# First norm of a two-block transformer kernel: weight row read from PSUM, real products ahead of the turns, shared squares

## The chip, the cores and the metric

The kernel runs on one core of one Trainium2 chip. The metric is device time in microseconds, launch to end. The kernel before took 901.84 us (median of 3 runs, 901.46 to 902.21).

## The reference, cut to what matters

The whole program computes two stacked blocks on x of 512 tokens by 1024 channels, in float32. Only its first step bears on the change:

```
def rms_norm(x, gain, eps=1e-6):
    y = x * rsqrt(mean(x * x, axis=-1, keepdims=True) + eps)
    return y * gain

h = rms_norm(x, pre_norm_gain)       # 512 x 1024, gain: one row of 1024
proj = h @ w_in                      # 1024 x 4096, eight parts of 512 columns
q, k, v, z_a, b_gate, c_gate, u, z_c = split(proj, 8)
...                                  # differential attention, gated convolution,
                                     # output product, norms, a gate, then a second block
```

The part v is computed first, because it is wanted with tokens on the partitions.

## The kernel before, in words

**Numbers in two halves.** Every large product is made nearly exact with three products of rounded operands: each operand is split into a high half (fp32r) and a low half (the rest). The helper `exact` (L2033) issues high x high, high x low and low x high into one PSUM bank. A block of k tiles of 128 channels is therefore 3k matmuls of 128x128 by 128x512.

**Weights.** They come in units of 2048 columns per partition, each in two halves of 1024. SyncE loads the halves into `raw`; GpSimd (POOL) makes `whi` by a copy (L836) and `wlo` by a subtraction (L843), two instructions of 512 columns each for a half. For the very first half ScalarE makes `whi` instead (L964). `w_lo` counts halves whose low part is ready. There are two slots for split units, so POOL waits for TensorE to finish with unit n before it splits unit n+2.

**The first stage.** x is loaded in four tiles of 128 tokens (`x_load`, L690), in between the first weight halves: x0, w0, x1, x2, w1, x3, w2, w3. Per tile t:

- ScalarE squares both halves of 512 channels with a row sum (`square_x`, L956, instruction L942).
- POOL adds the two sums and raises to -1/2 (`root`, L781; L791 and L794), giving `rstd`.
- VectorE multiplies x by `rstd` and by the gain row in one instruction a half (`normed_x`, L1422; L1428) into `tok`, which holds two tiles in turn.
- TensorE turns `tok` with four transposes a half into a PSUM bank (`turn`, L2108; L2120), so that channels lie on the partitions.
- ScalarE copies the bank to `actA_hi` (`turned`, L945; L953), and VectorE writes the rest to `actA_lo` (`rest`, L1383; L1394). `lo["x"]` counts these.
- TensorE computes the block of v for the tile. It is cut in three: `("Th", "v", 0, 0, t)`, the first two channel tiles of weight unit 0, whose weights are split first; `("T", "v", 0, 0, t)`, the other two, which need the second half of the unit; and `("T", "v", 0, 1, t)`, four channel tiles of unit 1.

**The gain row.** ScalarE's first instruction loads the row of `pre_norm_gain` to one partition (L961). TensorE spreads it to 128 partitions by a product with a row of ones, one matmul with one row for each half (`gn`, L2209), and VectorE copies the two PSUM banks to `gain[:, 0]` (L1419). Only then does it norm. Between, TensorE does twelve transposes of the identity (`warm`, L2212), whose result is used by nothing.

**Order.** Each engine works in program order. TensorE's is the list of `tensor_order` (L188): blocks wait for what `ready` (L2123) names, and for the bank to be emptied (`bank_of`, L253, and `emptied`, L555). In the first stage it is: gn0, gn1, warm, and per tile the two turns, then from tile 2 on `T` of tile t-2, then `Th` of tile t; after that T of tiles 2 and 3, the four blocks of unit 1, and the blocks for q and k. POOL's order is: root 0; low part of half 0; root 1; high part of half 1; root 2; its low part; root 3; the halves of unit 1; and so on. VectorE's and ScalarE's orders are written out in the code below. A memset of two pad columns (L1409) raises `pads_made`, which ScalarE waits for when it copies the first convolution input.

## Time and profile before

| | |
|---|---|
| median of 3 runs | 901.84 us |
| profiled execution | 902.16 us |
| its span, first to last instruction | 900.4 us |
| mean granted TensorE clock | 0.993 |
| TensorE busy | 875.2 us, 97% |
| VectorE, ScalarE, GpSimd busy | 542.6, 356.4, 556.4 us |
| in the first 2 to 14 us: TensorE, VectorE busy | 10.99, 8.52 us |

The profile is one execution. Engines are PE (matmul), PEld (its weight load), DVE (VectorE), ACT (ScalarE), POOL (GpSimd) and SP (SyncE). A line as L843 is a line of the kernel; a helper's line stands for all its callers. "out<-in" names the tiles. In a timeline the bracket at the end says how long the engine was idle before the instruction and what released it. Matmuls overlap, so the distance between two starts, and not the duration, is what one costs.

### The profile page before, as it was taken

The page shows a single profiled execution, that of the slowest core. Times are in us where ns is not written, and L with a number is a line of the kernel's source. Part 1 is how long each engine was busy: PE and PEld are TensorE (multiplying, and loading weights), DVE is VectorE, ACT ScalarE, POOL GpSimd, SP SyncE. Part 2 cuts the span into 40 slices and gives each one's busy share as a digit, 9 for nine tenths or more (in the row PEclk, how much of TensorE's full clock was granted, in tenths as well). Part 3 has the DMA queues.
Part 4 walks back from the last instruction along what each step waited for, and adds up shares of the span by engine and source line. Part 5 has one row for each costly group of instructions (what it writes and reads, how often), then busy time and mean ns, then how long its engine had stood idle before and what let it go on. Part 6 is the DMA issues. An engine that isn't in the chain of part 4 may idle for free.

```text
span 900.4 us, 11943 instructions
## 1 busy us (share of the span) xinstructions
PE 875.2 (97%) x4224; PEld 727.0 (81%) x4224; DVE 542.6 (60%) x878; ACT 356.4 (40%) x792; POOL 556.4 (62%) x620
## 2 busy tenths in 40 slices
PE   8999999999999999999999999999977999999997
PEld 5888888888888777888888888888866988888886
DVE  6125647775035489676766625556975457878624
ACT  5124332431134367545112311123634436766622
POOL 7766556576789832318974058762397798556352
PEclk9999999999999999999999999999998999999999
DMA  7443231332422467895742254327932122211202
GB/s 198 140 129 103 71 91 50 94 140 89 133 83 94 142 129 164 212 219 167 175 126 90 75 165 122 111 94 178 223 115 69 47 95 71 71 48 62 80 1 94
DMA packets 81516, 102.65 MB, mean 114 GB/s; under 512 B 11825, under 2 KB 54321, under 8 KB 81458
## 3 DMA queue, kind: packets, MB, share of 16 engines
q1 hardware_dynamic: 72752, 85.12, 29.5%
q0 software_dynamic: 8704, 16.78, 11.0%
q8 instruction: 34, 0.56, 0.3%
q14 instruction: 24, 0.20, 0.1%
q10 hardware_dynamic: 2, 0.00, 0.0%
HBM read 99.79 MB, written 2.10 MB: 113 GB/s over the span
## 4 chain that ended last, share of the span: by engine, by line
PE 90%; POOL 5%; issue 2%; DVE 1%; ACT 1%; DMA 0%; POOLq 0%; DVEq 0%; ACTq 0%
PE bank L2036 27%; PE bank L2037 27%; PE bank L2038 27%; PE bank L2264 2%; PE bank L2292 1%; PE bank L2120 1%; POOL wlo L843 1%; PE bank L2237 1%; PE bank L2287 1%; PE bank L2286 1%; POOL tok L813 1%; POOL raw L813 1%; DVE tok L1428 1%; POOL v5lo L843 1%; ACT junk L942 1%
## 5 line engine op out<-in xcount | busy, mean ns | idle before, releaser
L843 POOL TENSOR_TENSOR wlo<-raw,whi 128x512 fp32r<-128x512 f32 x204 | 280.8, 1407 | 0.1
L836 POOL TENSOR_SCALAR whi<-raw 128x512 fp32r<-128x512 f32 x202 | 141.8, 738 | 185.4 <-PE bank L2038 176.4
L2036 PE MATMUL bank<-actB_hi,whi 128*128 128x512 f32 (+1 forms) x416 | 159.5, 383 | 2.3 <-POOL wlo L843 2.3
L2037 PE MATMUL bank<-actB_lo,whi 128*128 128x512 f32 (+1 forms) x416 | 158.6, 381 | 0.0
L2038 PE MATMUL bank<-actB_hi,wlo 128*128 128x512 f32 (+1 forms) x416 | 158.5, 381 | 0.0
L2036 PE MATMUL bank<-whi,actA_hi 128*128 128x512 f32 x320 | 128.5, 402 | 6.7 <-DVE wlo L1702 5.0
L2037 PE MATMUL bank<-wlo,actA_hi 128*128 128x512 f32 x320 | 126.2, 394 | 0.0
L2038 PE MATMUL bank<-whi,actA_lo 128*128 128x512 f32 x320 | 126.2, 394 | 0.0
L2036 PEld LDWEIGHTS bank<-actB_hi,whi 128*128 128x128 f32 x416 | 78.2, 188 | 17.5 <-issue 2.9
L2038 PEld LDWEIGHTS bank<-actB_hi,wlo 128*128 128x128 f32 x416 | 78.2, 188 | 15.1
L2037 PEld LDWEIGHTS bank<-actB_lo,whi 128*128 128x128 f32 x416 | 78.3, 188 | 14.1
L2036 PE MATMUL bank<-actA_hi,whi 128*128 128x512 f32 x224 | 87.9, 392 | 0.0
L2037 PE MATMUL bank<-actA_lo,whi 128*128 128x512 f32 x224 | 87.3, 390 | 0.0
L2038 PE MATMUL bank<-actA_hi,wlo 128*128 128x512 f32 x224 | 87.3, 390 | 0.0
L2036 PEld LDWEIGHTS bank<-whi,actA_hi 128*128 128x128 f32 x320 | 61.0, 191 | 21.5 <-DVE wlo L1702 5.2
L2038 PEld LDWEIGHTS bank<-whi,actA_lo 128*128 128x128 f32 x320 | 61.1, 191 | 13.1
L2037 PEld LDWEIGHTS bank<-wlo,actA_hi 128*128 128x128 f32 x320 | 61.1, 191 | 12.4 <-issue 0.2
L2036 PE MATMUL bank<-whi,actB_hi 128*128 128x512 f32 x144 | 56.4, 392 | 0.0
L2038 PE MATMUL bank<-whi,actB_lo 128*128 128x512 f32 x144 | 56.1, 390 | 0.0
L2037 PE MATMUL bank<-wlo,actB_hi 128*128 128x512 f32 x144 | 56.0, 389 | 0.0
L1735 DVE TENSOR_TENSOR acc<-acc,gcv 128x512 f32<-128x512 f32 x16 | 15.6, 972 | 58.4 <-ACT gcv L1213 58.4
L2038 PEld LDWEIGHTS bank<-actA_hi,wlo 128*128 128x128 f32 x224 | 42.0, 188 | 8.9
(262 smaller groups left out, 1593.7 us busy)
## 6 DMA issues: line engine op xcount, KB each, us to landing
raw<-in_a_w_in SPq DMA_DIRECT2D x44, 512.0 KB, 4.3
raw<-in_w_in SPq DMA_DIRECT2D x32, 512.0 KB, 3.8
raw<-in_b_w_in SPq DMA_DIRECT2D x16, 512.0 KB, 3.4
raw<-in_a_w_out SPq DMA_DIRECT2D x12, 512.0 KB, 3.4
gain<-in_a_w_out POOLq DMA_DIRECT2D x9, 512.0 KB, 8.6
raw<-in_w_out SPq DMA_DIRECT2D x8, 512.0 KB, 4.0
raw<-in_w_ple_gate SPq DMA_DIRECT2D x8, 512.0 KB, 3.3
gain<-in_a_w_in POOLq DMA_DIRECT2D x8, 512.0 KB, 7.7
```

The source lines that it names most:

```text
L813: pool.tensor_scalar(src[:, k * 256:(k + 1) * 256], src[:, k * 256:(k + 1) * 256], g[:, 4 * h + k:4 * h + k + 1], 1.0, ALU.mult, ALU.mult) ...
L836: pool.tensor_scalar(H, src[:, i * HALF:(i + 1) * HALF], 1.0, 1.0, ALU.mult, ALU.mult).then_inc(w_hi, 1)
L843: ins = pool.tensor_tensor(L, src[:, i * HALF:(i + 1) * HALF], H.bitcast(f32), ALU.subtract)
L942: A(junk[:, :], src, ACT.Square, scale=1.0 / 32, accum_out=ss[:, NORMS[name], t, c:c + 1])\
L1428: V.scalar_tensor_tensor(tok[:, t % 2, half], resid[:, t, half], rstd[:, NORMS["x"], t:t + 1], gain[:, 0, half], ALU.mult, ALU.mult).then_ ...
L1735: V.tensor_tensor(acc[:, f % 2, :], acc[:, f % 2, :], gcv[:, f % 2, 0:S], ALU.mult).then_inc(zu_made, 1)
L2036: M(out_, whi_, xhi_, start=start, stop=False)
L2037: M(out_, whi_, xlo_, start=False, stop=False)
L2038: return M(out_, wlo_, xhi_, start=False, stop=stop)
L2120: ins = nc.tensor.transpose(bank[:, k * P:(k + 1) * P], src, ident[:, :])
L2237: ins = M(bank[:, qt * P:(qt + 1) * P], wgtT1[:, k * P:(k + 1) * P], tile(vtok, k)[:, h * P:(h + 1) * P], start=k == 0, stop=k == qt)
L2264: ins = M(bank[:, n * P:(n + 1) * P], big[:, n, f * P:(f + 1) * P], wcT[:, (f // 2) * P:(f // 2 + 1) * P], start=True, stop=True)
```

## The change

It touches the first stage alone.

1. VectorE first sets all of `gain[:, 1]` (128 x 1024) to zero; ScalarE's DMA of the gain row waits for that. The two broadcasts multiply a 128 x 128 matrix of ones with the 128 rows, of which all but the first are zero. Their result stays in PSUM (banks 7 and 3), and the norm reads it there; the two copies are gone.
2. In place of the twelve transposes there are ten f32 matmuls of the identity with 128 columns of ones: four ahead of the broadcasts, two behind them, four behind tile 0's `Th`.
3. Tiles 0 and 1: ScalarE squares the first half, VectorE the second (a reduce of both operands in SBUF, with its own semaphore). Tiles 2 and 3: ScalarE squares both, as before. ScalarE's order is new: square 0, weight copy, turned (0,0), square 1, turned (0,1), square 2, turned (1,0), square 3, turned (1,1), then the rest.
4. `Th` of tile t stands ahead of `T` of tile t-2. `Th` of tile 0 waits separately for the high half of the activations, then for their low half, and takes its two products with the low weights last.
5. The turns of x use three banks instead of four, so that bank 3 stays free for the gain row.

```diff
@@ -188,11 +188,11 @@
 def tensor_order():
 
     o = []
-    o += [("gn", c) for c in range(2)] + [("warm",)]
+    o += [("warm", 0)] + [("gn", c) for c in range(2)] + [("warm", 1)]
     for t in range(T):
         o += [("tr", "x", t, j) for j in range(2)]
+        o += [("Th", "v", 0, 0, t)] + ([("warm", 2)] if t == 0 else [])
         o += [("T", "v", 0, 0, t - 2)] if t >= 2 else []
-        o += [("Th", "v", 0, 0, t)]
     o += [("T", "v", 0, 0, t) for t in (2, 3)]
     o += [("T", "v", 0, 1, t) for t in range(T)]
     o += [("F", "q", f) for f in range(4)] + [("F", "k", f) for f in range(4)]
@@ -255,7 +255,7 @@
     kind = b[0]
     if kind == "tr":
         name, t, j = b[1:]
-        return {"x": (2 * t + j) % 4, "p": 4 + j, "x1": t + 4 * j, "h": (2 * t + j) % 4,
+        return {"x": (2 * t + j) % 3, "p": 4 + j, "x1": t + 4 * j, "h": (2 * t + j) % 4,
                 "n": (2 * t + j) % 4}[name]
     if kind in ("F", "Fa", "Fk"):
         s, f = b[1:]
@@ -278,7 +278,7 @@
         return BANKS_A[UNITS_A[b[1]][0]] + b[2]
     if kind == "s4":
         return 4 * (b[1] // 2 % 2) + b[1] % 2
-    return {"gn": lambda c: 6 + c, "warm": lambda: 3, "sc": lambda i, m: 4 + m, "tw": lambda i: 6, "pv": lambda i: 7, "ta": lambda h: 6,
+    return {"gn": lambda c: (7, 3)[c], "warm": lambda n: 6, "sc": lambda i, m: 4 + m, "tw": lambda i: 6, "pv": lambda i: 7, "ta": lambda h: 6,
             "ple": lambda t, c: t + 4 * c, "wt": lambda j: 4 + j, "rw": lambda j: 6 + j,
             "v5": lambda t: 4 + t % 2, "s5": lambda s, m: 4 + m, "t5": lambda s, kt: 6 + kt,
             "o5": lambda s: 3}[kind](*b[1:])
@@ -498,6 +498,7 @@
 
 
         x_in = [sem(f"x_in{t}") for t in range(T)]
+        x_squared = sem("x_squared")
         raw_in = [sem(f"raw_in{n}") for n in range(6)] + [sem(f"{n}_added{h}") for n in ("t3", "t") for h in range(2)]
         raw_in += [sem(f"room_in{h}") for h in range(2)]
         small_in, gain_in = sem("small_in"), [sem(f"gain_in{g}") for g in range(3)]
@@ -591,7 +592,7 @@
             a = b[1]
             if kind == "t5":
                 return (pt_lo[1], a + 1) if b[2] else (pt_lo[0], kt0_steps(a))
-            return {"gn": (base_step, 4 + a), "sc": (scored, 2 * a + b[-1] + 1), "tw": (wt_copied, a + 1),
+            return {"gn": (tok_ready["x"], 7 + a), "sc": (scored, 2 * a + b[-1] + 1), "tw": (wt_copied, a + 1),
                     "pv": (attn_copied, a // 4 + 1), "ta": (attn_out, a + 1),
                     "ple": (squared["e"], 2 * a + b[-1] + 1), "wt": (wct_copied, a + 1),
                     "rw": (rw_copied, a + 1), "s4": (s4_scaled, a + 1), "v5": (v5_lo, a + 1),
@@ -782,7 +783,9 @@
 
                 n = NORMS[name]
                 nth = next(roots)
-                pool.wait_ge(squared[name], T + t + 1 if name in BY_HALF else t + 1 if name == "ln" else 2 * (t + 1))
+                if name == "x" and t < 2:
+                    pool.wait_ge(x_squared, t + 1)
+                pool.wait_ge(squared[name], (1, 2, 4, 6)[t] if name == "x" else T + t + 1 if name in BY_HALF else t + 1 if name == "ln" else 2 * (t + 1))
                 m = ms[:, n, t:t + 1]
                 if name == "ln":
                     pool.tensor_scalar(m, ss[:, n, t, 0:1], 1.0 / width, EPS, ALU.mult, ALU.add)\
@@ -938,6 +941,8 @@
                 value = T * c + t + 1 if name in BY_HALF else 2 * t + c + 1
                 if name == "a":
                     value = SQUARES_A.index((t, c)) + 1
+                if name == "x":
+                    value = t + 1 if t < 2 else 2 * t - 1 + c
                 last_square[:] = squared[name], value
                 A(junk[:, :], src, ACT.Square, scale=1.0 / 32, accum_out=ss[:, NORMS[name], t, c:c + 1])\
                     .then_inc(squared[name], 1)
@@ -955,19 +960,24 @@
 
             def square_x(t):
                 act.wait_ge(x_in[t], 16)
-                for c in range(2):
+                for c in range(1 if t < 2 else 2):
                     square("x", t, c, resid[:, t, c * HALF:(c + 1) * HALF])
 
+            act.wait_ge(pads_made, 1)
             act.dma_start(gain[0:1, 1], pre_norm_gain[0:1, :]).then_inc(gain_in[0], 16)
             square_x(0)
             act.wait_ge(raw_in[0], LANDED[0, 0])
             A(halves_of(0, 0, 2)[0], raw[:, 0, :], ACT.Copy).then_inc(w_hi, 2)
+            turned("x", 0, 0)
             square_x(1)
-            for t in range(T):
+            turned("x", 0, 1)
+            square_x(2)
+            turned("x", 1, 0)
+            square_x(3)
+            turned("x", 1, 1)
+            for t in range(2, T):
                 for j in range(2):
                     turned("x", t, j)
-                if t + 2 < T:
-                    square_x(t + 2)
 
             act.wait_ge(lam_step, 2)
             A(lams[:, 2:4], lams[:, 0:2], ACT.Exp).then_inc(lam_exp, 1)
@@ -997,7 +1007,7 @@
                         act.wait_ge(za_gated, f)
                     A(th[:, :], bank, ACT.Tanh, scale=0.5).then_inc(za_tanh, 1)
                 if s == "c":
-                    act.wait_ge(pads_made, 1)
+                    act.wait_ge(pads_made, 2)
                     if f >= 2:
                         act.wait_ge(conv_out, f - 1)
                     A(gcv[:, f % 2, 2:2 + S], bank, ACT.Copy).then_inc(c_copied, 1)
@@ -1406,6 +1416,7 @@
                     ins = V.scalar_tensor_tensor(tok[:, t % 2], resid[:, t], r, gain[:, g], ALU.mult, ALU.mult)
                 ins.then_inc(tok_ready[turn], 1)
 
+            V.memset(gain[:, 1], 0.0).then_inc(pads_made, 1)
             V.memset(gcv[:, :, 0:2], 0.0).then_inc(pads_made, 1)
 
             dve.wait_ge(consts_made, 5)
@@ -1414,10 +1425,12 @@
             V.scalar_tensor_tensor(base1, base1, -1.0, base1, ALU.mult, ALU.max).then_inc(base_step, 1)
             dve.wait_ge(base_step, 2)
             V.memset(base1[0:64, HALF - 64:HALF], MASKED).then_inc(base_step, 1)
-            for c in range(2):
-                dve.wait_ge(pe_block, BLOCK["gn", c])
-                V.tensor_copy(gain[:, 0, c * HALF:(c + 1) * HALF], psum[bank_of(("gn", c))][:, :])\
-                    .then_inc(base_step, 1)
+
+            def square_x(t):
+                dve.wait_ge(x_in[t], 16)
+                half = resid[:, t, HALF:D]
+                V.tensor_tensor_reduce(acc[:, t, :], half, half, 1.0 / D, 0.0, ALU.mult, ALU.add,
+                                       ss[:, NORMS["x"], t, 1:2]).then_inc(x_squared, 1)
 
             def normed_x(t):
                 dve.wait_ge(rstd_ready["x"], t + 1)
@@ -1425,19 +1438,25 @@
                     dve.wait_ge(pe_block, BLOCK["tr", "x", t - 2, 1])
                 for c in range(2):
                     half = slice(c * HALF, (c + 1) * HALF)
+                    dve.wait_ge(pe_block, BLOCK["gn", c])
                     V.scalar_tensor_tensor(tok[:, t % 2, half], resid[:, t, half], rstd[:, NORMS["x"], t:t + 1],
-                                           gain[:, 0, half], ALU.mult, ALU.mult).then_inc(tok_ready["x"], 1)
-
-            dve.wait_ge(base_step, 5)
+                                           psum[bank_of(("gn", c))][:, :], ALU.mult, ALU.mult)\
+                        .then_inc(tok_ready["x"], 1)
+
+            square_x(0)
             normed_x(0)
             rest("x", 0, 0)
+            square_x(1)
             rest("x", 0, 1)
             normed_x(1)
-            for t in range(1, T):
-                rest("x", t, 0)
-                if t + 1 < T:
-                    normed_x(t + 1)
-                rest("x", t, 1)
+            rest("x", 1, 0)
+            normed_x(2)
+            rest("x", 1, 1)
+            rest("x", 2, 0)
+            normed_x(3)
+            rest("x", 2, 1)
+            rest("x", 3, 0)
+            rest("x", 3, 1)
             dve.wait_ge(small_in, 16 * 13)
             for n in range(2):
                 V.tensor_tensor_reduce(lamv[:, 2 * n], lamv[:, 2 * n], lamv[:, 2 * n + 1], 1.0, 0.0,
@@ -2061,8 +2080,21 @@
                     ins = exact(out_, H[:, c], L[:, c], aH[:, k, :], aL[:, k, :], k == 0, k == KD - 1)
                 return ins
 
+            def first_head():
+                n = UNIT_NO["v", 0]
+                aH, aL = READS["v"]
+                bank = psum[bank_of(("T", "v", 0, 0, 0))][:, :]
+                for a_, w_, need in ((aH, whi, (w_hi, 2)), (aL, whi, (lo["x"], 1)), (aH, wlo, (w_lo, 1))):
+                    pe.wait_ge(*need)
+                    for k in range(2):
+                        ins = M(bank, a_[:, k, 0:P], w_[:, SLOT[n], k * HALF:(k + 1) * HALF],
+                                start=a_ is aH and w_ is whi and k == 0, stop=False)
+                return ins
+
             def token_major(stage, c, kh, t, head=False):
 
+                if head and (stage, c, kh, t) == ("v", 0, 0, 0):
+                    return first_head()
                 first = HEADS.get((stage, c, kh, t), 0)
                 H, L = weights_of(stage, 2 * c + kh, head and first <= 2)
                 aH, aL = READS[stage]
@@ -2144,7 +2176,9 @@
                         pe.wait_ge(lo["n"], T if kind == "Fa" else 2 * T)
                 if kind in ("T", "Th"):
                     c, kh, t = b[2:]
-                    if s == "v":
+                    if s == "v" and (kind, kh, t) == ("Th", 0, 0):
+                        pe.wait_ge(hi["x"], 1)
+                    elif s == "v":
                         pe.wait_ge(lo["x"], 2 * t + 1 + kh)
                     if s == "wo":
                         pe.wait_ge(*((lo["attn"], NH1 - (kind == "Th")) if kh == 0 else (lo["conv"], 4)))
@@ -2206,10 +2240,10 @@
                     return turn(*b[1:])
                 if kind == "gn":
                     pe.wait_ge(gain_in[0], 16)
-                    return M(bank[:, :], ones[0:1, :], gain[0:1, 1, b[1] * HALF:(b[1] + 1) * HALF], start=True, stop=True)
+                    return M(bank[:, :], ones[:, :], gain[:, 1, b[1] * HALF:(b[1] + 1) * HALF], start=True, stop=True)
                 if kind == "warm":
-                    for n in range(12):
-                        ins = nc.tensor.transpose(bank[:, (n % 4) * P:(n % 4 + 1) * P], ident[:, :], ident[:, :])
+                    for n in range((4, 2, 4)[b[1]]):
+                        ins = M(bank[:, n * P:(n + 1) * P], ident[:, :], ones[:, :], start=True, stop=True)
                     return ins
                 if kind in ("F", "Fa", "Fk"):
                     return feature_major(*b)
```

## Rows read from the trace of the kernel before

**Rows 1.** The page, part 4: chain that ended last, by engine.

```profile
PE 90%; POOL 5%; issue 2%; DVE 1%; ACT 1%; DMA 0%; POOLq 0%; DVEq 0%; ACTq 0%
```

**Rows 2.** Waits of PE, whole run: engine line, releaser, total, times, longest.

```profile
PE bank L2036 <- DVE wlo L1702: 5.0, 2, 4.7
...
PE bank L2209 <- DMA gain<-in_pre_norm_gain: 2.4, 1, 2.4
```

**Rows 3.** Timeline of PE, 0 to 26 us: start, us, then as the page.

```profile
2.44 3.75 PE L2209 MATMUL bank<-gain,ones 1*128 1x512 f32 x4 [2.44 <-DMA gain<-in_pre_norm_gain]
6.12 2.82 PE L2212 MATMUL bank<-ident 128*128 128x128 f32 x12
...
11.34 0.80 PE L2036 MATMUL bank<-whi,actA_hi 128*128 128x512 f32 x1
...
14.06 1.25 PE L2120 MATMUL bank<-ident,tok 128*128 128x128 f32 x8
16.29 0.50 PE L2036 MATMUL bank<-whi,actA_hi 128*128 128x512 f32 x1 [0.98 <-DVE actA_lo L1394]
...
17.78 0.60 PE L2120 MATMUL bank<-ident,tok 128*128 128x128 f32 x4
...
19.12 0.47 PE L2036 MATMUL bank<-whi,actA_hi 128*128 128x512 f32 x1
...
21.96 1.04 PE L2120 MATMUL bank<-ident,tok 128*128 128x128 f32 x8
```

**Rows 4.** Timeline of PE, 26 to 60 us: first q block.

```profile
39.20 0.39 PE L2036 MATMUL bank<-actA_hi,whi 128*128 128x512 f32 x1
```

**Rows 5.** Chain in order of time, 0 to 24 us: start, us, what.

```profile
0.79 1.51 DMA gain<-in_pre_norm_gain
```

**Rows 6.** Timeline of DVE, 0 to 14 us.

```profile
0.87 0.06 DVE L1409 MEMSET gcv<- 128x4 f32 x1 [0.87 <-PEq L2323]
...
3.49 0.11 DVE L1416 MEMSET smB<- 64x64 f32 x1
```

**Rows 7.** Timeline of DVE, 14 to 30 us.

```profile
15.54 0.69 DVE L1394 TENSOR_TENSOR actA_lo<-bank,actA_hi 128x512 fp32r<-128x512 f32 x1 [1.26 <-ACT actA_hi L953]
...
23.23 1.29 DVE L1394 TENSOR_TENSOR actA_lo<-bank,actA_hi 128x512 fp32r<-128x512 f32 x2 [1.06 <-ACT actA_hi L953]
```

**Rows 8.** Timeline of ACT, 0 to 50 us.

```profile
4.27 0.63 ACT L942 ACTIVATE junk<-resid 128x512 f32<-128x512 f32 x1 [1.65 <-DMA resid<-in_x]
...
8.09 0.63 ACT L942 ACTIVATE junk<-resid 128x512 f32<-128x512 f32 x1 [1.29 <-DMA resid<-in_x]
...
22.59 1.09 ACT L953 ACTIVATE actA_hi<-bank 128x512 fp32r<-128x512 f32 x2 [2.59 <-PE bank L2120]
```

**Rows 9.** Timeline of POOL, 0 to 14 us.

```profile
5.84 0.30 POOL L791 TENSOR_SCALAR ms<-ss 128x1 f32<-128x1 f32 x1 [3.62 <-ACT junk L942]
...
6.94 2.94 POOL L843 TENSOR_TENSOR wlo<-raw,whi 128x512 fp32r<-128x512 f32 x2
9.98 0.63 POOL L791 TENSOR_SCALAR ms<-ss 128x1 f32<-128x1 f32 x1
10.69 0.57 POOL L794 TENSOR_TENSOR rstd<-ms,mhalf 128x1 f32<-128x1 f32 x1
```

**Rows 10.** Timeline of POOL, 14 to 30 us.

```profile
25.10 2.54 POOL L843 TENSOR_TENSOR wlo<-raw,whi 128x512 fp32r<-128x512 f32 x2
```

**Rows 11.** Line L1428 alone: duration ns min/median/max, first and last start.

```profile
L1428 DVE SCALAR_TENSOR_TENSOR tok<-resid,rstd,gain x8: 744/961/1802, 7.0 to 20.5; 128x512 f32<-128x512 f32 x8
```

**Rows 12.** Line L1394 alone, 0 to 40 us.

```profile
L1394 DVE TENSOR_TENSOR actA_lo<-bank,actA_hi x8: 675/686/692, 10.6 to 23.8; 128x512 fp32r<-128x512 f32 x8
```

**Rows 13.** Groups of DVE by line and shape: busy us, mean ns, idle.

```profile
L1528 DVE CUSTOM_DVE_ANT_0 tok<-bank,smA 128x512 f32<-128x512 f32 x8 | 5.2, 689 | 4.3 <-PE bank L2228 4.1
```

**Rows 14.** Windows: stretch, length, busy us of PE, PEld, DVE, ACT, POOL, granted clock.

```profile
674.00:680.00 6.00, 5.93 (x14) 4.69 (x15) 3.27 (x5) 0.04 (x1) 5.65 (x11) 0.50 0.80 260
682.00:687.00 5.00, 1.82 (x16) 1.61 (x15) 1.89 (x3) 4.10 (x9) 4.10 (x6) 0.99 0.00 0
687.00:690.50 3.50, 3.50 (x19) 3.50 (x18) 2.91 (x4) 0.41 (x2) 2.17 (x3) 0.52 0.00 0
```

**Rows 15.** Waits of all engines, 28 to 900 us.

```profile
POOL whi L836 <- PE bank L2038: 176.4, 34, 37.9
```

## The prediction

> **What bounds the kernel now.** I read the chain that ended last first: 90% of the span is TensorE, which computes almost without a break [rows 1]. Then the waits of PE: the longest comes near 670 us, behind a VectorE split; one of 2.4 us stands at the very start, for the gain row [rows 2]. The change touches only the first 30 us, so I took the timeline there engine by engine. PE's list shows the two gain broadcasts, the twelve idle transposes, and then the steps of the four token tiles (turn, two blocks of six products) [rows 3]. From the turn of tile 3 at 21.96 us, which ends near 22.87, PE has no gap: exactly 72 products (24 of unit 0, 48 of unit 1) stand before the first q block at 39.20 us [rows 4], so 16.33 / 72 = 0.227 us each. POOL waits for PE, 176.4 us in all, in the splits behind it [rows 15]. So whatever the head gains or loses passes to the end, and the question is when those 72 products can run without a gap. For that I follow one clock: where tile 3's first product block lands.
>
> Clock level: the products from 11.34 to 14.06 us are six in 2.72 us, 0.43 us apart, the pace of 1.2 GHz; eight transposes then take 1.25 us and the next products run at the 0.23 us pace of 2.4 GHz, so the rise lies near 14.4 us [rows 3].
>
> **Part by part.**
>
> *Gain row.* ScalarE's DMA now waits for a VectorE memset of 128x1024. Two memsets give 0.06 us for 4 columns and 0.11 us for 64 [rows 6], a slope of 0.83 ns a column: 0.06 + 1020 x 0.83 ns = 0.91 us. It starts at 0.87, so the DMA is issued near 1.85 instead of 0.79. From issue to data took 1.51 us [rows 5]; that was before the x loads filled the queues. I add 0.3 for them: landed at 3.7. Bounds: 3.4 with nothing added, and 6.0 if it takes as long to land as x tile 0 (4.27 - 0.80, that is 3.5 us, from an issue at 0.80) plus some more. What is queued behind the waiting DMA on ScalarE is its table load and the first square; ScalarE sat idle 1.65 us before that square [rows 8], so 1.06 us of delay is covered. The memset itself stands ahead of nothing urgent: VectorE's next real work waits for POOL's iota until past 2.2 us.
>
> The Trainium skill (VectorE: DVE Perf Modes, "Zero memsets can be issued as uint32 (trn2)") says a memset takes one cycle per element; at its 0.96 GHz that would be an estimate of 1.07 us, and the landing 0.16 us later. No row here has a long memset; I keep the 0.91 of the two short ones.
>
> *Broadcasts and warm products.* PE can start at about 1.8 us, when the identity stands. Four 128-column f32 products at the low pace are a quarter of a broadcast each: a broadcast takes (6.12 - 2.44) / 2, about 1.75 us with latency taken off [rows 3], so 0.43 each and 1.7 in all; done at 3.5, hidden before the gain row. The broadcasts then run from 3.8. The first is readable about 2.1 us after its start (5.9), the second 1.7 later at the low pace (7.6) or less. They have 128 rows in place of one; I cost that at nothing, since the 128-row products of this trace keep to their columns.
>
> *Clock.* Stretches of dense products before a rise were 3.1 us here (11.34 to 14.4) and about 6.0 us after 674 us, where the granted clock is 0.50 over the whole stretch [rows 14]; the twelve idle transposes (2.82 us) and the K=1 broadcasts had not brought it [rows 3]. Products now run from 1.8 with a gap of 0.3, so the rise falls between 4.9 and 7.9. I take 6.3: the second broadcast is then readable at 7.1.
> The Trainium skill (TensorE: Matmul & The Clock Gate, "Part 4: PE-mode transpose") says that a transpose does not count as TensorE activity for the clock; by that rule the old twelve were idle for the gate and the new ten are work. The trace agrees as far as it goes: the pace after them was still low. If transposes counted like products, the new ones would bring the clock no sooner than the old ones did, and the sum would be the late rise of rival 2.
>
> *Squares shared.* Tile 0: both halves are done at 5.05 instead of 5.75; a VectorE reduce of this size takes 0.69 us with one operand in PSUM [rows 13]. POOL's root starts at 5.84 now [rows 9], so 5.1 then, and the scale is ready at 6.1. If the reduce with both operands in SBUF meets a POOL split it can take up to the 1.80 us of the normalization's worst case [rows 11]; tile 0's meets none, and tile 1's comes after the split of 6.94 to 9.88.
>
> *Norm from PSUM.* L1428 with its two SBUF tensors takes 0.74 to 1.80 us while POOL is splitting [rows 11]; L1394, which reads one operand from PSUM, takes 0.68 to 0.69 us always, POOL splitting or not [rows 12]. So the four norms need 0.7 us a half, and POOL's pair of splits 2.54 us [rows 10] in place of 2.94 [rows 9]; its small root step drops from 0.63 to 0.30.
>
> *The sum along the path.* Tile 0: norm halves at 6.15 and 7.2; turns at 7.2 and 8.0; copies at 7.9 and 8.6. A turn's copy starts 0.63 after it, VectorE's rest 0.64 after the copy [rows 3, 7, 8], and the product 0.75 after the rest starts (15.54 to 16.29) [rows 3, 7]. ScalarE then squares half of tile 1 (its x landed by 8.09 [rows 8]) at 8.4, VectorE the other half behind its rest at 9.1 to 9.9. Root: 10.0 to 10.95, against 9.98 to 11.26 [rows 9]. So tile 1's scale comes only 0.3 earlier: its squares are now queued behind tile 0's turns. Norm 11.0 (before: 12.9), turn 11.8, copy 12.5, rest 13.2 to 13.9, products (Th1) 13.9 against 16.29: 2.4 us gained. Th1 takes 6 x 0.227 = 1.37: turn of tile 2 at 15.3 against 17.78. Its rest ends 2.0 us later (0.63 + 0.64 + 0.75, a little more for the queue): Th2 at 17.4. Here the moved order costs. Before, the lower-half block T0 ran under that latency, from 19.12; now Th stands first and PE waits about 1.1 us, in tile 2 and again in tile 3. Th2 and T0 are 2.73 us: turn of tile 3 at 20.15 against 21.96, Th3 at 20.15 + 2.1 = 22.25. From there the 24 and 48 products are the same as those that stood at 22.87. The difference is 0.6 us; my walk with the old rows comes out 0.2 us late at this point, so I take 0.7. The last split of unit 1 ends at 24.2 by the same walk, against 27.64 before and PE's need at 27.5: it covers itself. If all the split work stayed as slow as now it would end about 26, still in time.
>
> The profiled execution took 902.16 us for a span of 900.42 (1.74 around it) and is 0.3 above the median of the runs. Minus 0.7 gives 901.46 on that one; a part of the 0.3 is likely the head of that execution, so I predict 901.3.
>
> **Rivals.**
> 1. *The gain row lands late* (other side, slower). Speaking for it: it is issued a microsecond later, into full queues. Against: it is 4 KB on its own queue. By the walk, landing at 5.0 costs 0.65 more, at 6.0 1.2 more; it turns a loss from about 5.1 on. Price at 6.0: 902.5.
> 2. *The clock comes up but does not stay, or comes late.* Between 10.6 and 13.9 PE has only four warm products and transposes. At 686.9 it fell after a stretch that held 16 short operations in 5 us [rows 14]; before, it had stayed up through 14.4 to 16.29. If Th1 to the tile-2 turn run at 1.2 GHz, 1.4 + 0.5 us are added, with no slack to take them up: 901.3 + 1.9 = 903.2. A rise only at Th0 and Th1 (12 to 15 us) gives 1.5 to 3 more, 902.8 to 904.2.
> 3. *No change to measure because only the clock's luck moves*: 901.8. The waits ahead of Th2 and Th3 then return all of the gain.
> 4. *More than forecast.* If the clock is up by 5 and POOL's first split (from 6.9, bound by the weight load) is the only limit, Th1 starts at 13.3 and the turn of tile 3 at 19.5: 0.5 to 0.6 more, 900.8; with earlier runs of the old head in a poor phase 900.0.
>
> **Numbers.** A change is told from none at about 0.2%, 1.8 us. Chances: forecast (900.6 to 902.0) 0.5; rival 1 0.1; rival 2 0.17; rival 3 0.1; rival 4 0.13. Faster than 900.04 needs the far end of rival 4: 0.1. Slower than 903.64 needs the far end of rival 2 or 1: 0.1. Within: 0.8. Range 900.0 to 903.2: it leaves out the last of rival 2 and of rival 4.
>
> **What would show it.** After: ScalarE's DMA issue at 1.8 to 2.0; first broadcast at 3.6 to 4.2; products at the 0.11 us pace for halves of 128 columns before 8 us; norms of 0.7 us each; PE idle for about 1.1 us before each of Th2 and Th3; first q block at 38.4 instead of 39.20. It is wrong if the q block starts more than 0.5 us away from that, and my reading of the moved blocks is wrong if PE does not wait ahead of Th2 and Th3.

## The result and the profile after

The changed kernel took 905.97 us (median of 6 runs, 904.42 to 906.83) against 902.03 us for the kernel before (6 runs, 901.46 to 903.75): ratio 1.0036, 95% interval 1.0025 to 1.0048. It is slower, beyond the upper end of the range. The profiled execution has a span of 905.1 us against 900.4.

TensorE's list of the changed kernel, from the start to the first q block (start, us, then as on the page), answers to [rows 3, 4]:

```profile
1.76 2.07 PE L2246 MATMUL bank<-ones,ident 128*128 128x128 f32 x8 [1.76 <-POOL ident L775]
6.08 3.78 PE L2243 MATMUL bank<-gain,ones 128*128 128x512 f32 x4 [2.25 <-DMA gain<-in_pre_norm_gain]
9.65 1.06 PE L2246 MATMUL bank<-ones,ident 128*128 128x128 f32 x4
10.50 1.59 PE L2152 MATMUL bank<-ident,tok 128*128 128x128 f32 x8
12.25 0.73 PE L2090 MATMUL bank<-whi,actA_hi 128*128 128x512 f32 x2 [0.15 <-ACT actA_hi L958]
...
15.42 1.38 PE L2152 MATMUL bank<-ident,tok 128*128 128x128 f32 x8 [0.36 <-DVE tok L1442]
17.49 0.50 PE L2055 MATMUL bank<-whi,actA_hi 128*128 128x512 f32 x1 [0.69 <-DVE actA_lo L1404]
...
19.00 1.03 PE L2152 MATMUL bank<-ident,tok 128*128 128x128 f32 x8
21.06 0.47 PE L2055 MATMUL bank<-whi,actA_hi 128*128 128x512 f32 x1 [1.02 <-issue]
...
23.89 1.03 PE L2152 MATMUL bank<-ident,tok 128*128 128x128 f32 x8
25.95 0.47 PE L2055 MATMUL bank<-whi,actA_hi 128*128 128x512 f32 x1 [1.02 <-issue]
...
42.38 0.39 PE L2055 MATMUL bank<-actA_hi,whi 128*128 128x512 f32 x1
```

The first q block starts at 42.38 instead of 39.20: 3.2 us are lost in the head. The broadcasts start at 6.08 instead of 2.44, after a wait of 2.25 us. From there everything is late: turns of tile 0 at 10.50, TensorE at the pace of 1.2 GHz up to 11.6 (two products in 0.73 us at 12.25 are at the 2.4 GHz pace; the broadcasts, 3.78 us for two, were not), Th1 at 17.49 against 16.29. Ahead of Th2 (21.06) and Th3 (25.95) PE idles 1.02 us each time. The moment of the rise is read from the pace here and below. The trace's list of granted clocks opens with the rise (11.62 us here, 14.49 in the kernel before), so a window earlier than that prints a clock of 1.00, which says nothing.

Where the row was, in the chain of the changed kernel in order of time, against [rows 5]:

```profile
1.08 0.91 DVE gain L1419
2.02 4.01 DMA gain<-in_pre_norm_gain
```

The memset costs 0.91 us, the load is issued at 2.02, and the row takes 4.01 us to land instead of 1.51.

VectorE of the changed kernel, against [rows 7, 11, 12]:

```profile
8.28 0.75 DVE L1442 SCALAR_TENSOR_TENSOR tok<-resid,rstd,bank 128x512 f32<-128x512 f32 x1 [3.37 <-PE bank L2243]
9.89 0.75 DVE L1442 SCALAR_TENSOR_TENSOR tok<-resid,rstd,bank 128x512 f32<-128x512 f32 x1 [0.87 <-PE bank L2243]
...
14.62 1.41 DVE L1442 SCALAR_TENSOR_TENSOR tok<-resid,rstd,bank 128x512 f32<-128x512 f32 x2 [0.49 <-POOL rstd L797]
```

Each half of the norm takes 0.75 us and two take 1.41, which is what one operand in PSUM was to bring; but the halves of tile 0 start at 8.28 and 9.89 (before: 6.95 and about 8.7), because each waits for its broadcast, and those come 3.6 us later.

POOL of the changed kernel, against [rows 9, 10]:

```profile
6.90 2.49 POOL L846 TENSOR_TENSOR wlo<-raw,whi 128x512 fp32r<-128x512 f32 x2 [0.83 <-ACT whi L970]
13.63 0.30 POOL L794 TENSOR_SCALAR ms<-ss 128x1 f32<-128x1 f32 x1 [4.24 <-DVE ss L1432]
```

The split is down from 2.94 to 2.49 us; the root of tile 1 is 3.65 us later than the 9.98 of before: POOL idles 4.24 us for tile 1's squares, which stand behind tile 0's turns in the orders of ScalarE and VectorE.

The other 1.5 us of the span are lost behind the first q block. Windows of the changed kernel (columns as [rows 14], then the share and the rate of the DMA engines), then of the experiment a_row_early, which is told below:

```profile
690.00:710.00 20.00, 18.09 (x122) 17.71 (x121) 10.41 (x13) 9.47 (x20) 14.46 (x23) 0.81 0.01 1
```

```profile
690.00:710.00 20.00, 15.73 (x130) 15.18 (x129) 10.38 (x14) 8.91 (x19) 14.45 (x24) 1.00 0.08 27
```

The granted clock in 690 to 710 us is 0.81 in one and 1.00 in the other. It is not the change alone that brings this: from the first q block to the end of the span the profiled executions of thirteen kernels fall in two groups, 861.0 to 861.6 us (ten of them, the kernel before with 861.2) and 862.5 to 862.7 (three: the changed kernel, b_row_late and x_norm_only, all with a clock under 0.92 in those 20 us). The kernel before itself spreads from 901.3 to 904.6 us over the 51 timed runs of the first two sets of experiments. Between 650 and 720 us the trace of each of those three holds 13.7 us at the lower clock; nine of the others hold 10.2 us and one, a_row_early, 6.8.

The timed runs show the same by their mean granted clock. Of 63 runs of the kernel before that list it, 34 have 0.991 and a median of 903.6 us, and 29 have 0.992 or more and a median of 901.7. How often the lower one comes differs between kernels (7 of 9 runs of b_row_late, 1 of 11 of a_row_early), and no run shows why. Among runs of 0.992 or more the changed kernel has a median of 905.1 us (4 runs), 3.4 above the 901.7 of the kernel before, and the first q block says 3.2. So I compare heads by the first q block and take the medians with this in mind.

### The profile page after: what moved, and what is told of

It is laid out like the page before. It is cut to its first block, busy times and chain, and to the rows that moved or that the text cites. A ratio compares the mean times of both kernels' runs of the same rounds, so it can differ in the third digit from the quotient of the medians.

```text
span 905.1 us, 11960 instructions
## 1 busy us (share of the span) xinstructions
PE 876.4 (97%) x4232; PEld 729.1 (81%) x4232; DVE 540.4 (60%) x881; ACT 354.7 (39%) x788; POOL 553.9 (61%) x620
## 4 chain that ended last, share of the span: by engine, by line
PE 89%; POOL 5%; issue 2%; ACT 1%; DVE 1%; DMA 0%; POOLq 0%; DVEq 0%; ACTq 0%
PE bank L2055 27%; PE bank L2056 27%; PE bank L2057 27%; PE bank L2298 2%; PE bank L2326 1%; PE bank L2152 1%; POOL wlo L846 1%; PE bank L2271 1%; PE bank L2321 1%; PE bank L2320 1%; POOL tok L816 1%; POOL raw L816 1%; POOL v5lo L846 1%; POOL rstd L797 1%; ACT junk L947 1%
## 5 line engine op out<-in xcount | busy, mean ns | idle before, releaser
L2055 PE MATMUL bank<-whi,actA_hi 128*128 128x512 f32 x318 | 126.6, 398 | 8.5 <-DVE wlo L1721 5.0
```

Of the source, the lines that this page charges most:

```text
L2055: M(out_, whi_, xhi_, start=start, stop=False)
```

## Experiments

The names: a_ are the changed kernel with something undone or, in a_quiet, with a wait added; b_ is the kernel before with something added; x_ and n_ have the early row and the old order of blocks. "q" is the start of the first q block in the profile. The ratio is to runs of the kernel before that were taken together with the run: their medians are 902.94 us for the set of a_row_early, a_old_order, a_early_old_order and b_row_late, 902.87 for that of a_one_row, a_quiet, x_norm_only and x_no_first_four, and 903.31 for the three n_ kernels.

| kernel | q, us | median, us (runs) | ratio to before, 95% |
|---|---|---|---|
| before | 39.20 | 902.03 (6) | |
| changed | 42.38 | 905.97 (6) | 1.0036 (1.0025 to 1.0048) |
| b_row_late | 41.84 | 906.29 (9) | 1.0035 (1.0023 to 1.0047) |
| a_one_row | 42.83 | 905.90 (4) | 1.0041 (1.0025 to 1.0057) |
| a_quiet | 41.63 | 904.58 (1) | |
| a_row_early | 40.44 | 903.26 (11) | 1.0006 (0.9997 to 1.0015) |
| a_old_order | 39.85 | 902.91 (11) | 1.0000 (0.9991 to 1.0010) |
| a_early_old_order | 37.84 | 901.33 (11) | 0.9986 (0.9976 to 0.9995) |
| x_norm_only | 37.63 | 900.80 (12) | 0.9979 (0.9969 to 0.9988) |
| n_one_square | 37.80 | 900.73 (6) | 0.9976 (0.9962 to 0.9989) |
| n_full_rows | 38.09 | 900.96 (7) | 0.9974 (0.9962 to 0.9986) |
| x_no_first_four | 36.84 | 900.22 (7) | 0.9975 (0.9964 to 0.9986) |
| n_no_warm | 36.52 | 899.47 (5) | 0.9962 (0.9949 to 0.9974) |

### The late row: undone, and alone

a_row_early:

```diff
-            act.wait_ge(pads_made, 1)
             act.dma_start(gain[0:1, 1], pre_norm_gain[0:1, :]).then_inc(gain_in[0], 16)
...
-            V.memset(gain[:, 1], 0.0).then_inc(pads_made, 1)
...
-                    return M(bank[:, :], ones[:, :], gain[:, 1, ...
+                    return M(bank[:, :], ones[0:1, :], gain[0:1, 1, ...
```

> The changed kernel with one thing undone: the gain row is loaded to one partition by ScalarE's first instruction, with no memset and no wait ahead of it, and the broadcasts use that one row. Order, warm products, shared squares and the norm from PSUM stay. Theory A (the row that lands at 6.0 us instead of 2.3 costs the 3.2 us by which the first q block moved, 42.35 against 39.20): first broadcast at 2.4 to 3.8, first q block at 38.4 to 39.7, time 3 us under the changed kernel, 902.0 to 903.0. Theory B (the moved order of the blocks and the squares queued behind the turns cost it, the row only took their cover): the q block stays above 41, time above 904.5.

b_row_late adds the memset and the wait to the kernel before:

```diff
+            act.wait_ge(pads_made, 1)
             act.dma_start(gain[0:1, 1], pre_norm_gain[0:1, :]).then_inc(gain_in[0], 16)
...
+            V.memset(gain[:, 1], 0.0).then_inc(pads_made, 1)
```

> The kernel before with one thing added: the memset of 128x1024 on VectorE and ScalarE's wait for it ahead of the gain row's DMA. Theory A: the DMA is issued at 2.0, lands at 6.0, broadcasts from 6.1, and the whole head slides: first q block at 41.5 to 42.5, time 904.5 to 905.5. Theory B: the copies and the idle transposes take up part of it, q block under 40.5, time under 903.5.

TensorE of b_row_late, then of a_row_early:

```profile
6.10 3.75 PE L2211 MATMUL bank<-gain,ones 1*128 1x512 f32 x4 [6.10 <-DMA gain<-in_pre_norm_gain]
...
41.84 0.39 PE L2038 MATMUL bank<-actA_hi,whi 128*128 128x512 f32 x1
```

```profile
3.76 3.78 PE L2241 MATMUL bank<-gain,ones 1*128 1x512 f32 x4
...
8.48 1.92 PE L2150 MATMUL bank<-ident,tok 128*128 128x128 f32 x8
...
15.59 0.50 PE L2053 MATMUL bank<-whi,actA_hi 128*128 128x512 f32 x1 [0.81 <-DVE actA_lo L1403]
...
19.14 0.47 PE L2053 MATMUL bank<-whi,actA_hi 128*128 128x512 f32 x1 [1.02 <-issue]
...
24.02 0.47 PE L2053 MATMUL bank<-whi,actA_hi 128*128 128x512 f32 x1 [1.02 <-issue]
...
40.44 0.39 PE L2053 MATMUL bank<-actA_hi,whi 128*128 128x512 f32 x1
```

Memset and wait alone put the kernel before at 41.84, 2.6 us later, and its median 3.35 us above the 902.94 of the runs beside it, as much as the changed kernel loses in ratio (1.0035 against 1.0036). Its q is what theory A had for it. Part of those 3.35 us is the mixture told above: 7 of its 9 runs have the mean clock of 0.991.

a_row_early gives 1.9 us back. Its q of 40.44 lies between the two theories (A: 38.4 to 39.7, B: above 41), so the row is a part of the loss of the changed kernel and not all of it. Nor is it as good as the kernel before, as its ratio of 1.0006 makes it look: among runs with a mean clock of 0.992 or more its median is 903.25 against 901.67, 1.6 us slower, and q says 1.2. With the row there, a_row_early still idles 1.02 us twice, and it starts its broadcasts at 3.76, because the four products ahead of them (from 1.75) hold PE. It also undoes two things at once, the late landing and the 128 rows. Against a_one_row, which has the late row and one-row broadcasts, the late landing alone is worth 42.83 - 40.44 = 2.4 us.

### The order of blocks

a_old_order, and a_early_old_order with both undone:

```diff
-        o += [("Th", "v", 0, 0, t)] + ([("warm", 2)] if t == 0 else [])
         o += [("T", "v", 0, 0, t - 2)] if t >= 2 else []
+        o += [("Th", "v", 0, 0, t)] + ([("warm", 2)] if t == 0 else [])
```

> The changed kernel with the order of blocks undone in tiles 2 and 3: T of tile t-2 stands ahead of Th of tile t again. The row still lands late. Theory A: the row decides when Th1 starts, so Th1 stays at 17.5, but the two idle stretches of 1.0 us ahead of Th2 and Th3 are filled by the T blocks: first q block at 39.8 to 40.5, time 2 us under the changed kernel, about 904. Theory C (the waits are only given back elsewhere, since the next turn waits for the norm): the q block stays within 0.5 us of 42.35.

> Both undone at once, early row and old order; left of the change are the norm from PSUM, the warm products and the shared squares. If the two costs add (my walk): first q block at 36 to 37.3, time 898.5 to 900.5, faster than the kernel before by 2 us. If they overlap: q block about 39, time 902.

TensorE of a_old_order:

```profile
7.01 3.67 PE L2243 MATMUL bank<-gain,ones 128*128 128x512 f32 x4 [3.18 <-DMA gain<-in_pre_norm_gain]
...
17.49 0.50 PE L2055 MATMUL bank<-whi,actA_hi 128*128 128x512 f32 x1 [0.69 <-DVE actA_lo L1404]
...
18.98 1.03 PE L2152 MATMUL bank<-ident,tok 128*128 128x128 f32 x8
...
39.85 0.39 PE L2055 MATMUL bank<-actA_hi,whi 128*128 128x512 f32 x1
```

Here the row landed even later (broadcasts from 7.01), Th1 starts at 17.49 as in the changed kernel, and q is 2.5 us earlier: the two waits of 1.02 us are gone. From the turn of tile 2 to Th2 it is now 0.79 us (18.98 to 19.77) and was 2.06, so each wait cost 1.27 us with its restart. Theory C falls, and theory A's q (39.8 to 40.5) is met; the median of 902.91 is 1.1 us under its 904. Both undone give 37.84, 4.54 us under the changed kernel against 1.94 + 2.53 = 4.47: the two costs add, although q is 0.5 us later than the walk had it (36 to 37.3) and the median, 901.33, above its 900.5.

That accounts for the loss at q: row and order of blocks cost 4.5 us together, and what is left of the change in a_early_old_order wins 1.4 (37.84 against 39.20), which leaves the 3.2.

### Why the row takes 4 us

a_quiet, one execution: SyncE holds all its loads until the row is there.

```diff
+            sp.wait_ge(gain_in[0], 16)
             x_load(0)
             load_half(0)
```

> The changed kernel with one wait added: SyncE issues its first x tile and all that follows only when the gain row has landed, so that the row finds empty queues. It splits the row's 4.0 us from issue to landing. Theory Q (it waits behind the x and weight packets): issued at 2.0, landed at 3.5, first broadcast at 3.8. Theory R (the wait is in the issue or in the row itself): landed near 6.0 again. The x tiles come 2.7 us later, so the whole is slower; only the landing is read.

Its chain in order of time, and its TensorE:

```profile
2.02 1.45 DMA gain<-in_pre_norm_gain
...
3.49 3.48 DMA resid<-in_x
```

```profile
3.62 2.59 PE L2244 MATMUL bank<-gain,ones 128*128 128x512 f32 x4
6.05 0.61 PE L2247 MATMUL bank<-ones,ident 128*128 128x128 f32 x4
9.69 1.31 PE L2153 MATMUL bank<-ident,tok 128*128 128x128 f32 x8 [3.03 <-DVE tok L1443]
```

In empty queues the row lands 1.45 us after its issue, as it did in the kernel before (1.51). So of the 3.7 us by which it is later, 1.2 are the memset and 2.5 are waiting behind the x and weight loads: theory Q. (In x_norm_only, where the row is issued at 0.79 and x tile 0 at nearly the same time, it took 2.40 us.)

### The height of the broadcast and the clock

a_one_row keeps the late row and undoes the 128 rows:

```diff
-                    return M(bank[:, :], ones[:, :], gain[:, 1, ...
+                    return M(bank[:, :], ones[0:1, :], gain[0:1, 1, ...
```

> The changed kernel with one operand shape undone: the memset and the wait stay, the row lands late, but the broadcasts use one row of ones and the one row of gains, as in the kernel before. Theory D (broadcasts over 128 rows are work that brings the clock up, over one row they are not): the products of tile 0 and the turns behind run at the 1.2 GHz pace beyond 11.6 us, the first q block moves from 42.4 to 43 or later, time at or above the changed kernel's 906. Theory E (the rows do not matter): rise at 11.6, q block at 42.4.

```profile
6.25 3.78 PE L2243 MATMUL bank<-gain,ones 1*128 1x512 f32 x4 [2.42 <-DMA gain<-in_pre_norm_gain]
...
10.97 1.91 PE L2152 MATMUL bank<-ident,tok 128*128 128x128 f32 x8
...
42.83 0.39 PE L2055 MATMUL bank<-actA_hi,whi 128*128 128x512 f32 x1
```

The eight transposes of tile 0 take 1.91 us, all at the low pace, against 1.59 in the changed kernel, and the rise comes at 13.5 us instead of 11.6; q is 0.45 us later, of which 0.17 are the row's own (6.25 against 6.08). That points to theory D, but q stays short of its 43 and the median (905.90) is that of the changed kernel. The difference is also no larger than what chance gives: a_old_order issues to TensorE the same work as the changed kernel until tile 2, has its broadcasts 0.9 us later, and its rise at 10.45, 1.2 us sooner. A wider gap lies between a_quiet and a_row_early, which both do the four products from 1.75 and start the broadcasts at 3.6 to 3.8: with 128 rows the two broadcasts took 2.59 us instead of 3.78, as the pace doubled within them, at 5.0 us; with one row it rose at 12.3. n_full_rows then gives 128 rows without the memset ahead of the load (edit against x_no_first_four below):

```diff
-            act.dma_start(gain[0:1, 1], pre_norm_gain[0:1, :]).then_inc(gain_in[0], 16)
+            act.dma_start(gain[0:32, 1], pre_norm_gain[0:1, :].to_broadcast([32, D])).then_inc(gain_in[0], 16)
...
+            V.memset(th[:, 0:P], 1.0 / 32).then_inc(pads_made, 1)
+            V.memset(gain[32:64, 1], 0.0).then_inc(pads_made, 1)
+            V.memset(gain[64:128, 1], 0.0).then_inc(pads_made, 1)
...
-                    return M(bank[:, :], ones[0:1, :], gain[0:1, 1, ...
+                    pe.wait_ge(pads_made, 3)
+                    return M(bank[:, :], th[:, 0:P], gain[:, 1, ...
```

> The fastest version so far with broadcasts over 128 rows that need no memset ahead of the load: the DMA writes 32 copies of the row to partitions 0 to 31, issued first, VectorE zeroes the other 96 meanwhile, and the left operand is 1/32 everywhere, so the sum over rows is the row. Theory D (full-height broadcasts bring the clock up, one-row ones do not): row at 2.8 to 3.5, the second broadcast or at the latest the turns of tile 0 at the 2.4 GHz pace, before 8.5 us, first q block at 35.4 to 36.2, time 899 to 899.7. Theory E (the height does not matter): rise near 11.6 as before, q block at 36.8 to 37.5.

```profile
0.79 3.88 DMA gain<-in_pre_norm_gain
```

```profile
4.76 3.75 PE L2245 MATMUL bank<-gain,th 128*128 128x512 f32 x4 [4.76 <-DMA gain<-in_pre_norm_gain]
...
9.15 1.09 PE L2153 MATMUL bank<-ident,tok 128*128 128x128 f32 x8
10.50 0.73 PE L2091 MATMUL bank<-whi,actA_hi 128*128 128x512 f32 x2 [0.25 <-ACT actA_hi L958]
```

The turns of tile 0 (1.09 us for eight) and its first products (0.73 for two) run at the 2.4 GHz pace (rise at 9.3), where x_no_first_four, the one-row version below, needs 1.91 and 1.22 (rise at 11.7). That is what theory D had of the clock, 0.8 us later than its 8.5. It does not hold for the time: 32 copies of the row take 3.88 us to land, the broadcasts start at 4.76, the first square of x tile 0 at 5.34 instead of 4.20, and q is 38.09, 1.25 later than in x_no_first_four and outside both theories. The clock earned about 1.3 us on TensorE (0.8 in the turns, 0.5 in the first two products) and the late data lost more.

### What carries the gain that is left

x_norm_only (the norm from PSUM, early row, old order; twelve transposes and ScalarE's squares as before). Besides the norm and its three banks it keeps, of the change, the separate waits of tile 0's `Th`:

> The norm from PSUM alone on the kernel before: early one-row load, twelve transposes behind the broadcasts, old order of blocks, all squares on ScalarE; the two copies are gone and the turns use three banks. If the norm from PSUM carries the gain of the version with early row and old order: first q block at 37.5 to 38.5, time 901 to 902. If it is the warm products and the shared squares that carry it: q block at 39.0 to 39.4, time as before.

```profile
7.01 2.82 PE L2234 MATMUL bank<-ident 128*128 128x128 f32 x12
9.62 1.36 PE L2140 MATMUL bank<-ident,tok 128*128 128x128 f32 x8
11.23 0.73 PE L2078 MATMUL bank<-whi,actA_hi 128*128 128x512 f32 x2 [0.25 <-ACT actA_hi L954]
```

Its clock rose within the turns, at 10.3 us (1.36 us for eight), after nothing but one-row broadcasts and idle transposes, sooner than in any other kernel with one-row broadcasts (the next are n_no_warm with 11.0 and a_early_old_order with 11.6). In the kernel before, with the same broadcasts 0.9 us earlier and the same transposes, it rose at 14.5. In b_row_late the last broadcast ended at 9.8, twenty transposes followed, and the clock rose behind them, at 14.7, ahead of the first product:

```profile
12.39 1.92 PE L2122 MATMUL bank<-ident,tok 128*128 128x128 f32 x8
14.86 0.50 PE L2038 MATMUL bank<-whi,actA_hi 128*128 128x512 f32 x1 [0.56 <-DVE actA_lo L1395]
```

So these runs do not show that the new products bring the clock sooner than the transposes did, which the forecast rested on; where the rise falls differs by 4 us between two kernels whose broadcasts and transposes are the same.

q is 37.63 and the median 900.80: this version is 1.6 us ahead of the kernel before at q, although its row came 0.9 us later. The early rise helps it, and one profile does not tell how much. n_one_square below has the norm from PSUM too, keeps the low pace through its first block (rise at 12.7), and is 1.4 us ahead. The norm from PSUM is therefore the likely source of the gain; next to a kernel before with an equally early rise it was not measured.

x_no_first_four is a_early_old_order without the products ahead of the broadcasts:

```diff
-    o += [("warm", 0)] + [("gn", c) for c in range(2)] + [("warm", 1)]
+    o += [("gn", c) for c in range(2)] + [("warm", 1)]
```

On it build n_one_square (ScalarE squares everything, and its order, POOL's waits and VectorE's list are those of the kernel before) and n_no_warm (no warm products at all). Of n_one_square, then of n_no_warm:

```diff
-                for c in range(1 if t < 2 else 2):
+                for c in range(2):
...
```

```diff
-    o += [("gn", c) for c in range(2)] + [("warm", 1)]
+    o += [("gn", c) for c in range(2)]
...
-        o += [("Th", "v", 0, 0, t)] + ([("warm", 2)] if t == 0 else [])
+        o += [("Th", "v", 0, 0, t)]
```

> Early one-row load and old order of blocks, with the norm from PSUM and the shared squares, and without the four products ahead of the broadcasts; there they held PE until 3.8 although the row had landed at 2.4. Broadcasts from 2.4, end 6.1, turn of tile 0 at 7.1 instead of 8.5; first q block 1.0 to 1.4 earlier than 37.84, at 36.4 to 36.9, time 900.0. If the four products are worth what they delay (the clock comes later without them): q block at 37.8 or later.

> The fastest version so far (early one-row load, old order of blocks, norm from PSUM, shared squares, six warm products, none ahead of the broadcasts) with the shared squares undone: ScalarE squares both halves of every tile, in the order of the kernel before. Theory S (the shared squares are no gain beyond tile 0, because they queue tile 1's squares behind tile 0's turns): tile 1's root starts at 9.7 instead of 10.25, first q block at 36.3 to 37.0 against 36.84, time within 0.1% of 900.2. Theory T (the share carries tile 0's earlier norm): q block 0.7 later, 37.5.

> The fastest version so far with all warm products left out (two behind the broadcasts, four behind tile 0's block). The turn of tile 0 can start at 6.2 instead of 7.1. Theory W (the products are worth the clock): the rise to 2.4 GHz comes after 12, tile 0's block and tile 1's turns run low, or the clock is low again at Th1; first q block at 37.5 or later. Theory V (with one-row broadcasts they only stand in the way): q block at 36.0 to 36.8, time 899.5 to 900.2.

TensorE of n_no_warm, and the chain of n_one_square:

```profile
3.24 3.75 PE L2241 MATMUL bank<-gain,ones 1*128 1x512 f32 x4 [3.24 <-DMA gain<-in_pre_norm_gain]
7.12 1.97 PE L2150 MATMUL bank<-ident,tok 128*128 128x128 f32 x8
...
12.08 1.38 PE L2150 MATMUL bank<-ident,tok 128*128 128x128 f32 x8 [0.57 <-DVE tok L1440]
14.16 0.50 PE L2053 MATMUL bank<-whi,actA_hi 128*128 128x512 f32 x1 [0.69 <-DVE actA_lo L1403]
...
36.52 0.39 PE L2053 MATMUL bank<-actA_hi,whi 128*128 128x512 f32 x1
```

```profile
1.69 5.91 DMA resid<-in_x
...
7.62 0.73 ACT junk L943 x2
...
8.37 0.72 ACT junk L943 x2
9.10 0.49 ACT actA_hi L954
```

Without the four first products q falls from 37.84 to 36.84. Without any it is 36.52, in spite of a row that landed 0.9 us later there, and the median of 899.47 is the best of all. The clock rose at 11.0, against 11.7 with the six products: with one-row broadcasts they only stand in the way (theory V). The last 0.3 us rest on one profile each, and the ratios of the two kernels (0.9975 and 0.9962) overlap in their intervals.

With the shared squares undone q is 37.80, 1.0 us later, more than theory T had and against theory S: x tile 1 lands at 7.6, and ScalarE's two squares of it (7.62, 8.37) then hold tile 0's copy until 9.10. The medians, 900.73 and 900.22, do not tell the two apart.

## Why the prediction was wrong

The forecast was 0.7 us less, with q at 38.4 (39.20 less the 0.7 of the sum is 38.5); it came out at 42.38. Nearly all of the miss lies ahead of Th1, which started at 17.49 and not at 13.9. From the measured Th1 the prediction's own steps, 1.37 + 2.1 + 2.73 + 2.1 + 16.33, give 42.1. By its own steps:

- **Gain row, the step that failed first.** Issue at 1.85 and a memset of 0.91 were right (2.02 and 0.91; the estimate by cycles had 1.07). "I add 0.3 for them: landed at 3.7" was not: the loads of x and the weights cost 2.5 (a_quiet against the changed kernel), and it landed at 6.0, the upper bound of the text. The late landing is worth 2.4 us at q in the changed kernel's form (a_one_row against a_row_early) and 2.6 us in the kernel before (b_row_late). I had the bound, took a value near the other end for "4 KB on its own queue", and gave the rival that said it 1 in 10.
- **Clock, the step that failed with it.** The rise was taken at 6.3 and came at 11.6. That explains the rest: a_row_early has its broadcasts at 3.76, where the forecast put them, and its q is still 2.0 us late (40.44), with the rise at 12.3 and the turns at 8.48 taking 1.92 us for eight, all low. But its broadcasts have one row. In a_quiet, with 128 rows and no gap between the four products and the broadcasts, the rise came at 5.0, even sooner than forecast; its x tiles are too late for its q to say anything. So the forecast of the clock may have been right for a row in time, and no run has 128 rows, the row in time and x in time together. "I cost that at nothing" is right for the time of the broadcasts (3.78 us for either height) and open for the clock.
- **Rival 1's price.** Landing at 6.0 was priced at 1.2 us with the clock's rise left where it was. The late row also opens a gap of 2.25 us between the four products and the broadcasts, and against a_quiet, which has no gap, the rise fell back from 5.0 to 11.6. Two terms that I had as separate rivals came together; that the gap is the cause rests on one profile of each.
- **Products ahead of the broadcasts.** "PE can start at 1.8" was right (1.76). The four took 1.9 to 2.0 us to the next start and not 1.7. They are "hidden" only behind a late row: once it lands by 2.4 they cost 1.0 us at q (37.84 against 36.84).
- **Order of blocks.** The price of 1.1 us for each of the two waits was right (1.02, and 1.27 with the restart). What was wrong is that I added them to a head that was to be 2.4 us ahead at Th1; that gain did not exist (17.49 against 16.29), so the 2.5 us were a loss with nothing to set against it.
- **Squares shared.** Tile 0's root at 5.1 was right (5.11), and so was that tile 1's squares now queue behind tile 0's turns; sharing gives 1.0 us at q once the row is early; no run undoes it with the late row.
- **Norm from PSUM.** 0.7 us a half and 2.54 us for the split: 0.75 and 2.49. Right, and likely the part that pays by itself (x_norm_only, with the reservation told there).
- **The rest of the program.** That the head's shift passes to the end was right: q to end is the same within 0.6 us in ten of thirteen kernels. The other three are 1.3 to 1.5 us longer with a clock of 0.81 to 0.91 in 690 to 710 us. I had taken the 0.75 us spread of three runs for the kernel's own; with 51 it is 3.3 us, and the medians here (902.0, 902.9, 903.3) move with it. Two slips changed nothing: the products behind tile 3's turn start at 22.75 and not 22.87 in the kernel before, and the far price of rival 2, 901.3 + 3, is 904.3.

The best version, n_no_warm, is ahead of both kernels: early one-row load, old order of blocks, norm from PSUM, shared squares, no warm products, ratio 0.9962 (0.9949 to 0.9974).

## What to carry to other kernels

Issue a small load that gates everything before the large ones: issued 1.2 us later, behind them, it landed 3.7 us later here. A price for "later by x" is to be taken with what else may hang on the same moment, here the clock. Work added to bring the clock up is to be measured against leaving it out: here it lost, 1.0 us at q for the four products ahead of the broadcasts and perhaps 0.3 for the other six. And where runs of one kernel differ by 3 us through a clock late in the run, a ratio of 1.00 does not say that a change of 1 us in the head is nothing.

## What the runs showed of the hardware

- The height of an operand does not change a product's time (3.75 us for the two broadcasts either way at the low pace). The granted clock rose sooner behind tall ones: counted from the start of the broadcasts to the rise in the trace, 1.4, 3.4, 4.5 and 5.5 us with 128 rows (a_quiet, a_old_order, n_full_rows, changed), 7.0 to 12.0 us with one row (the other nine profiles). One profile each, and the moment of the rise is uneven, so this is a pattern of thirteen runs and not a law.
- Transposes did not keep the clock low: in b_row_late it rose at 14.7 us, 4.9 us after the last broadcast had ended, with nothing but twenty transposes between.
- A 4 KB load on ScalarE's queue took 1.45 us with no other load in flight, 1.5 to 2.4 when issued together with the first large loads, and 3.9 to 5.0 (four profiles) when issued 1.2 us after them. In n_full_rows, issued early but as 32 copies, it took 3.88.
- The norm of 128x512, which took 0.74 to 1.80 us with both tensors in SBUF [rows 11], took 0.74 to 0.75 with one of them in PSUM (changed), and POOL's pair of splits went from 2.94 to 2.49 us.
